# Two attention blocks of a layer stack rebuilt: norms among the projection's products, output per head, scores two heads ahead

## What is computed

```python
def diff_attention(...):       # first block: 8 heads, q and k in two halves of 64
    q, k, v = split(h @ w_qkv, 3)
    q = rms_norm(q per 64 columns, q_gain) * 64**-0.5
    k = rms_norm(k per 64 columns, k_gain)
    s = q k^T + bias[bucket(distance)], causal;  p = softmax(s)
    a = p[half 0] - lam * p[half 1]
    o = rms_norm(a @ v, subln_gain) * (1 - lambda_init)      # per head of 128
    return o @ w_o
def sliding_window_attention(...):  # second block: 16 query heads, 4 key heads of 64
    q, k = partial_rope(rmsnorm(q)), partial_rope(rmsnorm(k))
    s = q k^T / 8, window 128;  p = softmax([s, sink]) without the sink
    return (p @ v) @ w_o
```

## Time and profile before

| | |
|---|---|
| median of 3 runs | 3406.84 us (3400.28 to 3407.38) |
| profiled execution, its own time | 3398.3 us |
| span of its records | 3396.5 us |
| TensorE matmul busy | 2978.7 us (88%) |
| VectorE busy | 2309.9 us (68%) |
| ScalarE busy | 1376.6 us (41%) |
| HBM traffic | 188 GB/s over the span |
| mean granted TensorE clock | 0.939 |

### The profile page before, as it was taken

The page is one execution under the profiler, slowest core; times in us unless marked ns, Lnnn a source line. Parts: engine busy times, 40 slices in busy tenths (PEclk is TensorE's granted clock), DMA queues, the critical chain, the costliest instruction groups (busy, mean ns, idle before and its releaser), DMA issues.

```text
span 3396.5 us, 48223 instructions
## 1 busy us (share of the span) xinstructions
PE 2978.7 (88%) x18518; PEld 2623.3 (77%) x18518; DVE 2309.9 (68%) x3190; ACT 1376.6 (41%) x1424; POOL 462.5 (14%) x244
## 2 busy tenths in 40 slices
PE   4998359999894599747999999999979999999999
PEld 3887147878784488626999998878768999998887
DVE  6887568875777555565797885556565978865565
ACT  3444234444444244323444344444434444344443
POOL 0300002202000011000485000000001880000000
PEclk9999569999997799968999999999989999999999
DMA  6786026765770145402455665667534555665675
GB/s 243 286 290 241 0 80 235 281 221 174 272 279 12 50 168 170 145 0 97 164 186 183 218 213 204 220 243 279 184 136 150 185 185 195 221 216 196 237 273 209
DMA packets 146886, 640.27 MB, mean 189 GB/s; under 512 B 12456, under 2 KB 46288, under 8 KB 90320
## 3 DMA queue, kind: packets, MB, share of 16 engines
q1 hardware_dynamic: 126928, 567.92, 48.4%
q10 hardware_dynamic: 19840, 70.79, 5.8%
HBM read 604.04 MB, written 34.62 MB: 188 GB/s over the span
## 4 chain that ended last, share of the span: by engine, by line
PE 80%; DVE 11%; DMA 4%; ACT 3%; issue 2%; SPq 0%; DVEq 0%; ACTq 0%
PE pp L443 23%; PE pp L445 11%; PE pp L581 7%; PE pp L582 7%; PE pp L583 7%; PE mz L647 6%; PE mz L649 6%; PE mz L650 6%; PE mz L623 3%; DMA raw<-expert_v 2%; DVE gsq L1136 2%; PE pp L491 1%; DVE w_lo L1039 1%; DMA ada_raw<-ada 1%; ACT w_hi L768 1%
## 5 line engine op out<-in xcount | busy, mean ns | idle before, releaser
L1039 DVE TENSOR_TENSOR w_lo<-raw,w_hi 128x2048 fp32r<-128x2048 f32 (+1 forms) x422 | 924.5, 2191 | 472.1 <-ACT w_hi L768 471.6
L768 ACT ACTIVATE w_hi<-raw 128x2048 fp32r<-128x2048 f32 (+1 forms) x486 | 894.0, 1840 | 557.6 <-DMA raw<-expert_v 370.7
L443 PE MATMUL pp<-hs,w_hi 128*128 128x512 f32 x2400 | 868.4, 406 | 41.1 <-DVE hs L1089 41.0
L445 PE MATMUL pp<-hs,w_lo 128*128 128x256 f32 x2400 | 679.6, 283 | 0.0
L443 PEld LDWEIGHTS pp<-hs,w_hi 128*128 128x128 f32 x2400 | 458.2, 191 | 166.3 <-issue 45.0
L581 PE MATMUL pp<-hs,w_hi 128*128 128x256 f32 x2048 | 585.5, 286 | 0.0
L582 PE MATMUL pp<-hs,w_hi 128*128 128x256 f32 x2048 | 579.9, 283 | 0.0
L583 PE MATMUL pp<-hs,w_lo 128*128 128x256 f32 x2048 | 579.8, 283 | 0.0
L1578 POOL TENSOR_TENSOR w_lo<-raw,w_hi 128x2048 fp32r<-128x2048 f32 x64 | 319.3, 5001 | 1157.3 <-ACT w_hi L768 1157.3
L445 PEld LDWEIGHTS pp<-hs,w_lo 128*128 128x128 f32 x2400 | 463.9, 193 | 0.0
L443 PE MATMUL pp<-us,w_hi 128*128 128x512 f32 x960 | 347.4, 406 | 80.2 <-DVE us L1147 74.5
(11 more groups left out here) (246 smaller groups left out, 3204.6 us busy)
## 6 DMA issues: line engine op xcount, KB each, us to landing
raw<-expert_u SPq DMA_DIRECT2D x128, 1024.0 KB, 4.9
raw<-expert_v SPq DMA_DIRECT2D x128, 1024.0 KB, 4.9
raw<-ffn_in SPq DMA_DIRECT2D x88, 1024.0 KB, 4.9
ada_raw<-ada ACTq DMA_DIRECT2D x120, 512.0 KB, 5.5
raw<-ffn_down SPq DMA_DIRECT2D x64, 704.0 KB, 5.0
raw<-out_w SPq DMA_DIRECT2D x16, 1024.0 KB, 4.9
raw<-hgrn SPq DMA_DIRECT2D x16, 1024.0 KB, 5.1
raw<-query SPq DMA_DIRECT2D x16, 1024.0 KB, 4.9
```

The source lines that it names most:

```text
L443: mm(outp, w_hi[:, slot, a:a + P], rhs[:, k0 + k].rearrange("p a t -> p (a t)"), start=(k0 + k == 0), stop=False, skip_group_check=True)
L445: last = mm(outp[:, 0:T], w_lo[:, slot, a:a + P], rhs[:, k0 + k, 0, :], start=False, stop=(k0 + k == last_k), skip_group_check=True)
L768: f(w_hi[:, slot, 0:n], raw[:, slot, 0:n], ACT.Copy).then_inc(hi_ready, 1)
L1039: v.tensor_tensor(w_lo[:, slot, 0:n], raw[:, slot, 0:n], w_hi[:, slot, 0:n].bitcast(F32), ALU.subtract)\
```

## The change

Both `group_norm` calls on q and k, the third one, `split_mix` and `attention` of the two blocks are replaced by functions of each block's own. In both projections squares, sums, spreading, transposes of v and rotations are put between the products of the chunks (keys come first now). The norms are summed in compact form: keys into a [16, 256] tile `k_inv`, which TensorE spreads over the partitions again with `pick_sb`, queries into a [128, 2, 16] tile `q_inv`, which is applied as a per-row scale with the bias (first block) or inside the exponential (second). The gain of q is folded into that of k, for the second block both into cosine and rotation tables. The bias table is prepared ahead of the first block. The mask of the second block is added by a bfloat16 matmul. The output of each head is normed in compact form (first block) or split directly from PSUM (second). The output product waits per tile (`tile_of_mix`).

TensorE, first block:

```diff
+                for rp, pair, half, lap in each_pair(ph):
+                    for j in range(2):
+                        c = 2 * rp + j
...
+                        if c == 1:
+                            pe.wait_ge(bias_done, 1)
...
+                        last.then_inc(w_used, 1)
+                        if 1 <= c <= 4:
+                            key_sums(c - 1)
+                        if 5 <= c <= 8:
+                            query_sums(c - 5)
+                        if 7 <= c <= 10:
+                            spread_keys(c - 7)
+                        if c >= 9:
+                            turn_values(c - 9)
+                turn_values(3)
...
+                score(0)
+                score(1)
+                pe.wait_ge(vt_copied, 4)
+                for h in range(HEADS):
+                    turn(h)
+                    if h + 2 < HEADS:
+                        score(h + 2)
+                    weigh(h)
+                    if h:
+                        head_sum(h - 1)
+                head_sum(HEADS - 1)
+                pe.wait_ge(o_inved, 1)
+                for k in range(KD):
+                    last = mm(pp[:, k // 4, (k // 2) % 2, (k % 2) * T:(k % 2 + 1) * T], pick_sb[:, k], o_inv[:],
+                              start=True, stop=True, skip_group_check=True)
```

The sums (two tiles at each step):

```diff
+                    for k in (2 * i, 2 * i + 1):
+                        last = mm(mz[0:2 * HEADS, 0, 0:T], halves[:, 14 - 2 * k:30 - 2 * k], gsq[:, k], start=(k == 0),
+                                  stop=(k == KD - 1), skip_group_check=True)
...
+                    for k in (2 * i, 2 * i + 1):
+                        for tb in range(TB):
+                            at_ = (1 - tb) * 2 * HEADS + 2 * k
+                            last = mm(mz[:, 3, at_:at_ + 2], gsq[:, k, tb * P:(tb + 1) * P], halves[:, 14:16], start=True,
+                                      stop=True, skip_group_check=True)
...
+                    for t in range(2):
+                        last = mm(mz[:, 1 + i % 2, t * T:(t + 1) * T], pick_sb[:, 2 * i + t], k_inv[:], start=True, stop=True,
+                                  skip_group_check=True)
```

VectorE, first block. `soft` becomes:

```diff
+                    for c in range(2):
+                        q1, q0 = (q_inv[:, i, 2 * h + c:2 * h + c + 1] for i in range(2))
+                        v.scalar_tensor_tensor(s1[:, c], pp[:, b, c, 0:T], q1, bias_t[:, h], ALU.mult, ALU.add)
+                        last = v.scalar_tensor_tensor(s0[:, c], pp[:, b, c, T:T + P], q0, bias_t[:, h, P:T], ALU.mult, ALU.add)
```

Second block, TensorE:

```diff
+                        mm(pp[:, b, c, 0:384], ident_b[:], band_b[:], start=True, stop=False, skip_group_check=True)
+                        mm(pp[:, b, c, 0:T], pj[r, 4 + h, P:T], pj[r, h // 4, :], start=False, stop=True, skip_group_check=True)
+                        last = mm(pp[:, b, c, T:T + P], pj[r, 4 + h, 0:P], pj[r, h // 4, 0:P], start=False, stop=True,
...
+                        if c == 1:
+                            key_sums()
+                            rotate(0)
+                        if c == 2:
+                            turn_values()
+                        if c == 4:
+                            spread_keys()
+                        if c >= 3:
+                            query_sums(c - 3)
+                            rotate(c - 2)
+                pe.wait_ge(evac_done, ph.evac0 + ph.evacs)
+                pe.wait_ge(sw_k_done, 1)
                 score(0)
+                query_sums(3)
+                rotate(4)
+                score(1)
                 for h in range(HEADS):
-                    if h + 1 < HEADS:
-                        score(h + 1)
                     turn(h)
-                    if h:
-                        weigh(h - 1)
-                weigh(HEADS - 1)
+                    if h + 2 < HEADS:
+                        score(h + 2)
+                    weigh(h)
```

Second block, ScalarE's and VectorE's ends of a head:

```diff
+                        f(scores[:, b, c, cols_], pp[:, b, c, cols_], ACT.Exp, bias=neg_max[:, b, n:n + 1],
+                          scale=sq_inv[:, i, 2 * h + c:2 * h + c + 1], accum_out=zsum[:, b, n:n + 1])
...
                for h in range(HEADS):
                    if h + 1 < HEADS:
                        expo(h + 1)
                    turned(h)
+                    if h:
+                        high(h - 1)
...
+                def low(h):
+                    dve.wait_ge(mix_hi, 2 * KD + h + 1)
+                    v.tensor_tensor(us[:, h, 1, :], mz[:, 2 + h % 2, 0:T], us[:, h, 0, :].bitcast(F32), ALU.subtract).then_inc(mix_lo, 1)
...
+                rope(3)
+                soft(0)
+                split_next(ph, rp, pair, half, j)
+                rope(4)
+                for h in range(HEADS):
+                    if h + 1 < HEADS:
+                        soft(h + 1)
+                    weights(h)
+                    if h:
+                        low(h - 1)
+                low(HEADS - 1)
```

More of the change, by code:

```diff
@@ L523, in turn @@
                         pe.wait_ge(pt_copied, n0 + h)
-                    for c in range(2 if wide else 1):
+                    for c in range(2):
                         src = probs_n[:, b, c]
@@ L541, in weigh @@
                     last.then_inc(o_ready, 1)
+                pe.wait_ge(rope_ready, 1)
+                pe.wait_ge(pick_in, 16)
+                pe.wait_ge(evac_done, ph.evac0)
+                for rp, pair, half, lap in each_pair(ph):
+                    for j in range(2):
+                        c = 2 * rp + j
+                        pe.wait_ge(lo_ready, 2 * pair + j + 1)
+                        pe.wait_ge(evac_done, ph.evac0 + c - 1)
+                        for t in range(2):
+                            last = tile_product(pp[:, j, t], 2 * half + j, t * KD, hs, 0, KD, KD - 1,
+                                                tile_of_h if c == t == 0 else None)
+                        last.then_inc(w_used, 1)
+                        if c == 1:
[8 more added lines that the diff above has]
+                            rotate(c - 2)
@@ L965, in _ @@
             norm(0, KD)
-            ffn(0, 0)
-            norm(1, KD - 1)
-            ph = plan[("attn", 0)]
-            products(ph)
-            act.wait_ge(w_used, 2 * (ph.pair0 + ph.pairs))
             act.wait_ge(bias_out, 16)
@@ new lines, in diff_projections @@
+            def diff_projections():
+                ph = plan[("attn", 0)]
+                for rp, pair, half, lap in each_pair(ph):
+                    for j in range(2):
+                        c = 2 * rp + j
+                        if c == 6:
+                            dve.wait_ge(k_rms, 1)
+                            v.reciprocal(k_inv[:], k_inv[:]).then_inc(k_inved, 1)
+                        add_halves(pj[:, 2 * c:2 * c + 2, :], ph.evac0 + c, j)
+                        split_next(ph, rp, pair, half, j)
+                        modulation(ph, rp, j)
+                        if 7 <= c <= 10:
+                            i = c - 7
+                            dve.wait_ge(k_wide, i + 1)
+                            keys_ = pj[:, 2 * i:2 * i + 2].rearrange("p k t -> p (k t)")
+                            v.scalar_tensor_tensor(keys_, keys_, gain[:, 0:1], mz[:, 1 + i % 2], ALU.mult, ALU.mult).then_inc(k_done, 1)
+                        if c == 10:
+                            dve.wait_ge(q_rms, 1)
+                            v.reciprocal(q_inv[:], q_inv[:]).then_inc(q_inved, 1)
+                dve.wait_ge(evac_done, ph.evac0 + ph.evacs)
+                dve.wait_ge(q_inved, 1)
@@ L1631, in shape_constants @@
     bucket[buckets(255 - np.arange(T)), np.arange(T)] = 1.0
-    return c, masks, bucket
+    pick = np.zeros((2 * HEADS, KD, P), np.float32)
+    for j in range(2 * HEADS):
+        pick[j, j // 2, 64 * (j % 2):64 * (j % 2) + 64] = 1.0
+    return c, masks, bucket, pick
 def kernel(**inputs):
```

571 lines of the change are left out of this document (399 added, 172 removed).

## The result

The changed kernel takes **3271.57 us** (median of 4 runs, 3265.4 to 3276.48) beside 3404.47 of the kernel before in the same comparison: ratio **0.961** (95% interval 0.9594 to 0.9627), 132.9 us less. Forecast were 3269 and 138.2. The profiled execution is the fastest of the four, 3265.4 us.

The account below looks back on a forecast made before the run. Bound: two blocks' serial norms and head rings, 294.5 us after the last products. −90.0 + 11.8 − 67.4 + 6.8 + 0.6 = −138.2, giving 3269 us against median 3406.84; range 3245 to 3302.

Parts of the forecast that it names:

- Reciprocals: VectorE's reciprocal of a 128x2048 norm, 12.95 us, in series four times in the two blocks and once at quarter width.
- Flip: First block, stage before: flip after the bias transfer, between two TensorE instructions, ends about 262.3; cost 0, bounds 0 and +2.
- Helpers, first block: Between projection products: key sums 3.4, key spreading 3.4, query sums 3.9, value transposes 1.0, paid in full; +11.8 us.
- First weights of the blocks: VectorE's first head weights are done 12.7 us (first block) and 14.1 us (second) after the last product.
- First ring: First block's heads: TensorE and VectorE stay in a closed ring; 6.75 us per head at low clock, 5.5 at high, 6.4 taken.
- (d): First block: scores really come two heads ahead, VectorE never waits; 4.7 a head, −10, 3259 us; chance 0.04.
- Behind the first heads: First block, last head to first output tile: eight spreads, 0.8 each at low clock, faster at the end; tile ends at 70.6.
- Second ring: Second block's heads: 7.9 us per head at the low clock, 5.7 at 2.4 GHz; 6.6 taken as mostly high.
- Prologue: Further input transfer and some 1.7 us of small VectorE work before the first modulation column; +0.6 us, bounds 0 and +2.
- (b): Helpers wait in TensorE's stream, 2 to 4 us in about 15 helpers; +30 to +60, 3300 to 3329 us; chance 0.12.
- (c): Projection stream turns serial, each helper waiting for its own chunk's round, some 8.2 us; 148 us in all, 3417; chance 0.02.
- (a): Heads go faster with TensorE staying at 2.4 GHz, periods 5.5 and 5.7; −5.4 per block, 3258 us; chance 0.12.

Follow-up runs that it names:

- experiment 6: The kernel before, with the reciprocals of its five wide norms in the two blocks left out (output differs): 3345.99 us, 0.984.
- experiment 2: The changed kernel with score(h+2) ahead of transpose(h) instead of behind it, in both blocks: 3251.91 us, 0.957.
- Experiment 4: The changed kernel with the first block's eight output-norm spreading matmuls on 128 rows in place of 16: 3266.76 us, 0.9609.
- experiment 3: The changed kernel, second block only, with both mask matmuls of a head ahead of its four 64-row score matmuls: 3261.57 us, 0.9587.
- experiment 9: The changed kernel with two unread 128-row matmuls ahead of each head's transposes in the first block (output differs): 3260.2 us, 0.958.
- experiment 7: The kernel before, with the pair loop of the first block's projection written out on every engine: 3398.5 us, 0.9993.
- experiment 5: The changed kernel without the norms of q and k in the first block (output differs): 3256.49 us, 0.9582.

## Why the prediction was right, step by step

- **Where the time lies.** The earlier trace rows held the gain, and it was carried to the end: blocks −127.9 measured, −138.8 forecast (−78.2 and −60.6 with their helpers); it was too hopeful by 10% and 5%, 10.9 us together, and 5 us that no edit explains came from elsewhere. So the sum's closeness (132.9 against 138.2) is partly luck.
- **Reciprocals.** As said: some 55 us in experiment 6.
- **Flip.** Cost 0, as said: it ended at 262.9 against 262.3, and the products then waited for hs, their input, up to 266.5.
- **Helpers, first block.** +14.8 against +11.8, within the range. Mis-sized were the key sums (4.5 against 3.4) and the spreads of keys (4.8 against 3.4), both priced by how long four records are busy, and not by how far they move the next product; and the slower pace (1.3) was put at nothing. Query sums measured 3.4 against 3.9. The second block's helpers measured +7.3 against +6.8.
- **First weights of the blocks.** 12.6 and 14.7 us after the last product, against 12.7 and 14.1.
- **First ring.** At the low clock 6.63 against 6.75, at the high one 5.54 against 5.5, six periods 38.65 against 38.4. The reading that the ring stays closed (rival (d) refused) is shown by experiment 2.
- **Behind the first heads.** The first output tile ended at 75.3 against 70.6. This step failed in size. Of the 4.7 us, 1.4 lie ahead of the spreads (they began at 62.8, forecast 61.4). The rest is "faster at the end": the spreads took 7.2 in place of 5.6, at the low clock throughout, and the first 5.3 us of products went at it too. Experiment 4, with 128 rows, got 2.4 of the 4.7 back.
- **Second ring.** Mean 7.13 against 6.6. Three terms failed. The halves in series cost 1.57 each at the low clock, not 1.28, so the period at the low clock is 8.48, not 7.9. At the high clock it is 6.04, not 5.7 (experiments 4 and 5). And "90% busy at the low clock, so mostly high" did not hold: TensorE was busy 8.30 of the first period's 8.48 us at 0.50, the granted clock was 0.72 over these heads, and in experiment 2 a stretch with TensorE busy 23.40 of 26.10 us stood at 0.54. The mask between the halves cost 8.1 us by experiment 3, against "up to 6", a part of it by way of the clock. The Trainium skill, "TensorE: Matmul & The Clock Gate", Part 3, has matmuls that use different parts of the array run concurrently. The traces agree for neighbours in the queue (1.59 us for both halves) and not with a 128-row matmul between them (1.57 for each).
- **Prologue.** −0.1 against +0.6: the first norm's reciprocal starts at 54.3 in place of 54.4.
- **Rivals.** (b) and (c) have nothing for them: TensorE never waited inside the projections. (a) was not what happened: both rings changed between the two clocks. In experiment 9 filled pauses brought the first ring most of the way. (d) was false of the change and true of experiment 2, with 4.2 to 4.3 a head in place of its 4.7.

Left open: why products run at 0.347 us a pair in some stages and 0.353 in others. The same stage, unedited, has gone at either (experiment 7), and neither helpers (experiment 5) nor the loop (experiment 7) is the cause. Also open is what sets the clock in a ring that neither fills nor leaves TensorE.

## What to carry to other kernels

To see how far ahead a stage really runs, don't count instructions: go round the ring and ask which queue entry the wanted result stands behind. In this kernel one swap of two lines in an issue order, with the wait that it needs, was worth 14 to 20 us by the whole times (11.6 in the first block by its trace). And where two engines take turns, look for a third behind whose copy one of them stands (low behind ScalarE, weigh behind the copy of the transposes): taking such steps one head later cost nothing that these runs show and, together with the scores further ahead, the halves side by side and the high clock that came with them, halved the second period, 7.1 to 3.3.

## What the hardware showed that was not expected

- Matmuls on 16 rows neither raised nor held TensorE's clock: 7.19 us of them without a pause stayed at the low level in six traces, in experiment 9 the clock fell from the high level within them, while the same eight on 128 rows brought the clock up (6.52, one trace) or kept it (3.72, one trace).
- TensorE's busy share did not tell its clock: 23.40 of 26.10 us busy stood beside 0.54 in experiment 2, 17.82 of 26.80 beside 1.00 in experiment 3.
- Two 64-row matmuls ran side by side only where they were neighbours in the queue: one 128-row matmul between them cost a whole half, 1.57 us at the low clock.
